# Moving eight adaLN blocks from layer 0's routing to behind its experts

## The reference: what is computed

```python
mod = ada_mod(c, w_ada[i], b_ada[i])                      # silu(c) @ w_ada[i] + b: 6 vectors of 1024
h = modulate(rmsnorm(x, norm_mix[i]), mod[:, 0], mod[:, 1])
x = x + mod[:, None, 2] * mixer(h)
h = modulate(rmsnorm(x, norm_ffn[i]), mod[:, 3], mod[:, 4])
x = x + mod[:, None, 5] * moe(h, w_router, b_router, w_exp_gate[i], w_exp_up[i], w_exp_down[i])
```

## Time and profile before

| | us |
|---|---|
| median of 3 runs | 1343.18 (1340.71 to 1351.53) |
| the profiled execution | 1344.42 |
| its span | 1342.8 |
| PE busy | 1213.2 (90%) |
| DVE, ACT, POOL busy | 371.9, 316.8, 122.9 |
| moved by DMA | 389.56 MB, 290 GB/s over the span |

### The profile page before, as it was taken

One profiled execution on the slowest core, in us unless ns is written; L12 is line 12 of the kernel. 1 busy time (PEld: TensorE's weight loads), 2 busy tenths in 40 slices (PEclk: granted clock), 3 DMA queues, 4 the chain that ended last, 5 costly groups with the idle time before them and its releaser, 6 DMA issues.

```text
span 1342.8 us, 24595 instructions
## 1 busy us (share of the span) xinstructions
PE 1213.2 (90%) x10356; PEld 702.6 (52%) x10356; DVE 371.9 (28%) x1138; ACT 316.8 (24%) x716; POOL 122.9 (9%) x188
## 2 busy tenths in 40 slices
PE   4787998789999989899989999999899987789996
PEld 2345544346886545555547743446465544565544
DVE  1246111250003522611122023341441115551113
ACT  1131111240123531211124211230311114401113
POOL 3001010210000000111120000000002111001111
PEclk8799998999999999899989999999999997989998
DMA  8999999795226793789979223891679989439993
GB/s 316 412 385 421 381 406 421 299 351 174 94 94 243 266 366 107 305 341 409 407 282 354 82 94 104 349 361 64 238 278 421 415 351 363 186 120 410 398 397 137
DMA packets 89707, 389.56 MB, mean 290 GB/s; under 512 B 10456, under 2 KB 38604, under 8 KB 53240
## 3 DMA queue, kind: packets, MB, share of 16 engines
q1 hardware_dynamic: 71568, 336.61, 64.2%
q0 software_dynamic: 17456, 51.07, 10.4%
q10 hardware_dynamic: 568, 0.23, 0.1%
HBM read 370.96 MB, written 27.96 MB: 297 GB/s over the span
## 4 chain that ended last, share of the span: by engine, by line
PE 77%; DMA 10%; DVE 5%; SPq 2%; issue 2%; ACT 2%; POOL 1%; ACTq 0%; POOLq 0%; DVEq 0%
PE bank L478 70%; DMA sb_ring<-in_w_ada 3%; PE bank L941 2%; SPq L435 2%; DMA sb_ring<-in_w_exp_up 2%; DMA slot_out<-sb_arena,sb_homes 1%; DMA sb_ring<-in_w_exp_gate 1%; DMA sb_arena<-slot_out,sb_slots 1%; PE bank L992 1%; PE bank L959 1%; POOL sb_arena L2078 1%; DMA slot_out<-sb_arena 1%; DMA sb_arena<-token_rows,sb_rows 1%; PE bank L874 0%; DVE sb_xT L1937 0%
## 5 line engine op out<-in xcount | busy, mean ns | idle before, releaser
L478 PE MATMUL bank<-sb_ring,sb_arena 128*32 128x256 f32 (+1 forms) x6112 | 460.3, 432 | 18.6 <-DMA sb_ring<-in_w_exp_down 6.4
L478 PEld LDWEIGHTS bank<-sb_ring,sb_arena 128*32 128x32 f32 x6112 | 226.7, 112 | 192.2 <-issue 109.4
L478 PE MATMUL bank<-sb_ring,sb_hT 128*128 128x256 f32 x624 | 142.3, 390 | 6.2 <-ACT sb_hT L1193 6.2
L478 PE MATMUL bank<-sb_arena 128*128 128x128 f32 (+8 forms) x728 | 127.9, 354 | 10.1 <-DVE sb_arena L1826 6.3
L478 PEld LDWEIGHTS bank<-sb_ring,sb_hT 128*128 128x128 f32 x624 | 121.6, 196 | 28.8 <-issue 10.5
L478 PE MATMUL bank<-sb_ring,sb_cond 128*2 128x512 f32 x768 | 104.4, 670 | 18.0 <-DMA sb_ring<-in_w_ada 17.6
L478 PEld LDWEIGHTS bank<-sb_arena 128*128 128x128 f32 (+2 forms) x728 | 90.0, 180 | 43.6 <-issue 13.3
L478 PE MATMUL bank<-sb_arena,sb_ring 128*128 128x384 f32 (+2 forms) x288 | 95.5, 507 | 3.0 <-DVE sb_arena L1678 2.1
L1892 DVE TENSOR_TENSOR sb_arena<-sb_arena,bank 128x256 f32<-128x256 f32 x40 | 16.9, 422 | 274.4 <-PE bank L478 274.4
L478 PE MATMUL bank<-sb_hT,sb_ring 128*128 128x384 f32 x256 | 82.9, 486 | 0.0
L478 PEld LDWEIGHTS bank<-sb_arena,sb_ring 128*128 128x128 f32 (+1 forms) x288 | 49.9, 181 | 44.9 <-issue 19.0
(11 more groups left out here) (310 smaller groups left out, 1029.5 us busy)
## 6 DMA issues: line engine op xcount, KB each, us to landing
sb_ring<-in_w_ada SPq DMA_DIRECT2D x96, 1024.0 KB
sb_ring<-in_w_exp_gate SPq DMA_DIRECT2D x60, 1024.0 KB
sb_ring<-in_w_exp_up SPq DMA_DIRECT2D x60, 1024.0 KB
sb_ring<-in_w_exp_down SPq DMA_DIRECT2D x60, 1024.0 KB
sb_ring<-in_w_mlstm_in SPq DMA_DIRECT2D x12, 1024.0 KB
token_rows<-sb_arena POOLq DMA_DIRECT2D x12, 512.0 KB, 4.7
slot_out<-sb_arena POOLq DMA_DIRECT2D x9, 512.0 KB, 8.5
sb_scratch<-in_w_exp_gate SPq DMA_DIRECT2D x4, 1024.0 KB
```

Of the source, the lines that this page charges most:

```text
L478: return pe.matmul(out, lhsT, rhs, start=first, stop=last)
```

## The change

Group 3 leaves `ADA_WINDOW[0]` and goes to a new table, `ADA_BEHIND[0]`. In the list of units its eight blocks now stand behind the 45 entries of layer 0's experts, and `hold` moves on by eight entries, so that it still falls on the first block of layer 1's mixer. PE does the group inside norm 2: four blocks ahead of the squares, once six of the eight rows of xT are ready; one between the squares and the second sum; three behind it, then the columns. ACT copies the bank after norm 2's 1/sqrt, and DVE makes `mod` and `amp` directly ahead of norm 2's scaling.

```diff
-        ADA_WINDOW = [(3,), (7,), (11,), ()]
+        ADA_WINDOW = [(), (7,), (11,), ()]
+        ADA_BEHIND = [(3,), (), (), ()]
...
-            hold[len(units) + 3 * (NE - 1)] = (yg_in[NT - 1], 32 * (L + 1))
+            hold[len(units) + 3 * (NE - 1) + KC * len(ADA_BEHIND[L])] = (yg_in[NT - 1], 32 * (L + 1))
...
             assert len(units) == moe_first[L] + 3 * (NE - 1)
+            ada_units(*ADA_BEHIND[L])
...
-            def norm(n):
+            def norm(n, groups=()):
+                for g in groups:
+                    pe.wait_ge(x_ready, 8 * n + 6)
+                    ada(g, 0, 1, 2, 3)
                 for k in range(KC):
...
                 ins.then_inc(ms_full, 1)
+                for g in groups:
+                    ada(g, 4)
                 pe.wait_ge(sq_ready, 6 * n + 6)
                 mm(ps[6][:, 0:TOK], mean_ones[:, 32:32 + P], rstd[:, :], True, True).then_inc(ms_full, 1)
+                for g in groups:
+                    ada(g, 5, 6, 7)
+                    ada_columns(g)
...
-                    norm(2 * L)
+                    norm(2 * L, ADA_BEHIND[L - 1])
...
                     norm_scale(2 * L)
+                    for g in ADA_BEHIND[L - 1]:
+                        mod_rows(g)
                 act.wait_ge(mod_added, 3 * L + 1)
...
+                if L:
+                    for g in ADA_BEHIND[L - 1]:
+                        mod_columns(g)
                 norm(2 * L, amp[:, L, 0, :, :])
```

## The result

The changed kernel takes 1365.24 us (1364.54 to 1366.06, 4 runs) against 1342.88 us (1340.71 to 1351.53, 4 runs) for the kernel before on the same chip: a ratio of 1.015, 95% interval 1.0123 to 1.0177, +22.4 us. Timed again beside each other later, the same pair gave 1361.53 (1357.61 to 1368.04, 4 runs) and 1342.38 us (7 runs), 1.0119 (1.006 to 1.0178), +19.2 us. Forecast were 1360.1 us and +16.9. The profiled execution took 1366.06 us, its span is 1364.4.

The account below looks back on a forecast made before the run. The chain that ended last was taken as 77% TensorE and 10% DMA. Terms -4.1 + 0 + 14.5 + 6.5 = +16.9 us on the profiled 1344.4 gave 1361.3, less 1.2 for the median: 1360.1 us, range 1348 to 1367.

Parts of the forecast that it names:

- case A: The forecast itself, all four terms as costed, 66%; own range 1356 to 1366 us.
- Term 1: Layer 0's routing, first position matmul to round 2's gates, gets shorter without the adaLN blocks: -4.1 us (-2.5 to -4.9).
- Term 2: Late gate block ahead of round 8: the 5.0 us wait stays, since loads hang on ring releases; 0 us.
- term 4: Norm 2 of layer 0 pays for group 3's blocks and columns ahead of its scaling: +6.5 us (5.8 to 8).
- term 3: Expert-output gathers behind layer 0's experts share DMA with w_ada; last lands at 280.2, not 265.7: +14.5 us.
- case E: Worse, 5%: w_ada also too late for norm 2, or clock low through it; +22 or more, 1365 to 1370 us.
- the transfer from layer 3: Layer 0's routing stage was to run like layer 3's, which has no adaLN there: 38.70 us instead of 42.84.
- The four blocks ahead of the router: Layer 0, before routing: they end about when hT's last row is ready, so removing them was costed at nothing.
- the dry stretch: DMA at 340 GB/s from 150 to 165 us: queue nearly dry, no early backlog left, loads then follow PE's rounds.
- The even split in bytes: Gathers beside w_ada get half the DMA bytes, not a third: +7.5 us instead of +14.5.
- Rival C: Gathers lose less, 11%: even share of the engines (+7.5) gives 1353.1 us, mere latency (+3.7) 1349.3.

Follow-up runs that it names:

- the kernel before with small blocks: Kernel before, with group 3's eight blocks in their old place but loaded as 64 KB each instead of 1 MB; 1343.48 us, ratio 0.9989.
- the first experiment: Changed kernel, with group 3's eight blocks loaded as 64 KB each instead of 1 MB, the engines' work kept; 1351.59 us, ratio 1.0048.
- the two 1 KB runs: Kernel before without layer 0's hold, mixer weights beside the gathers, 1348.52 us; changed kernel with the eight blocks in 1 KB packets, 1371.35 us.
- under the hold: Changed kernel with hold eight entries earlier, on group 3's first block, so w_ada loads behind the gathers; 1364.96 us, ratio 1.0145.
- the last kernel: Changed kernel with 1 KB packets, four blocks at a time, sixteen matmuls in the routing gap, aside expert's loads at round 4; 1346.84 us, ratio 1.0046.
- the four-group kernel: Changed kernel with group 3's blocks in 1 KB packets, taken four at a time so PE goes round four column groups; 1358.28 us, ratio 1.0118.

## Why the prediction was right or wrong

**Direction and main mechanism were right.** The time is within the range, case A is what happened, and the gathers carry it. The forecast is not saved by terms that cancel: terms 1 and 2 were together 2.6 us too good, term 4 was 1.0 too small, term 3 right. The size was 17 forecast and 19 to 22 measured, the trace's own sum at layer 1's start being 20.4. At 1365.24 us the time also touches case E's, but not by its mechanism: PE waits for no block of w_ada in norm 2, and the clock is back at 0.94 from 284 to 289 us.

**Term 1, -4.1, came out at -1.4.** From the first position matmul to round 2's gates are 144.74 - 103.33 = 41.41 us, 42.84 before. The step that failed is the transfer from layer 3, where the stage takes 38.70. In all seven traces of kernels with this gap left empty layer 0's stage takes 40.7 to 41.7 us. The 2.7 us between them are two things of like size. The idle gap is the same (5.44, 5.45), but the clock was down earlier and for longer, 0.50 over 104 to 112, where the like stretch of layer 3 (1173 to 1181) has 0.60: the picks begin 9.16 us behind the first position matmul and last 9.16, in layer 3 8.24 and 8.46, 1.6 us more. And the token fetch, with 6.06 us shorter than the 9.30 of the earlier trace rows, was still waited for, 1.35 us, though DMA moved only 196 GB/s then; in layer 3 PE doesn't wait for it. One row of another layer didn't bound the phase of the clock, and my bound of -2.5 was too narrow. Of the -1.5 us that are left at POOL's first gather the changed kernel had -1.2 already at the first position matmul (103.33 against 104.53), from 24 matmuls of the mixer near 54 us (6.32 us against 7.62) that the change doesn't touch. The four blocks ahead of the router, put at nothing, did cost nothing: from 60.34 (61.54 before) to the first position matmul both kernels take 42.99 us.

**Term 2, 0, held as to its mechanism.** The wait stays, even with w_ada's bytes gone, and the dry stretch is there again (348 GB/s from 150 to 165, 340 before). It grew from 5.0 to 7.2 us, and the block's way from issue to landing from 16.35 to 18.55. PE's lead was waited away there: it came to the wait at 223.99 - 7.2 = 216.8, before at 224.4 - 5.0 = 219.4, 2.6 us sooner, and left it 0.4 sooner. Why the block doesn't land sooner in proportion stays open (in the kernel before with small blocks it landed 5.1 us sooner, at 219.10, after round 2 had begun 5.2 sooner); the wait was 5.9 us in the first experiment, which has 0.5 MB of w_ada behind it, so the eight blocks' bytes aren't needed for it. The clock behind the wait was 0.74, not 0.50, from 224 to 229, hence 8.35 us of matmuls instead of 9.39.

**Term 3, +14.5, measured +14.4.** Rate and start were right: 1.68 and 0.82 MB in 6 us are 280 and 137 GB/s, forecast from the earlier trace rows were 275 and 138. The landing was forecast at 280.2 and came at 278.61. In the second trace of the changed kernel the gathers take 25.2 us, not 26.6, so about 1.4 us of the term are chance. The even split in bytes that I weighed against the row is refuted by the two 1 KB runs; counted in the profile's packets, the Trainium skill's rule of turns (DMA: Bandwidth & Descriptors, Queues, rings and completion order) is what the traces show. What I didn't see is that w_ada is needed for norm 2 as well. Two kernels let the gathers land early, and won 2.5 and 1.5 us at the scaling. Rival C was priced as if the gain of faster gathers were kept; in these two it was not. Gathers and w_ada together are 8.4 + 2.9 = 11.3 MB, 27 us at 417 GB/s, so from POOL's first gather at 252.03 both can't have landed before about 279 (an estimate, and the changed kernel comes close to it). That bound alone doesn't explain the small gains: in the two kernels w_ada's last block landed at 291.02 and 287.85, 12 and 9 us behind it, since the engines were not full (244 GB/s from 252 to 264 us under the hold; 350 to 354 from 265 to 285 with 1 KB packets). From the last block's matmuls to the scaling are 4.2 us under the hold (291.06 to 295.25). Whether an order exists that gets near 279 + 4 = 283 wasn't tried.

**Term 4, +6.5, measured +7.5.** The four blocks ahead of the squares: the last gather landed to the second mean matmul is 292.32 - 278.61 = 13.71 us, 9.56 before, so +4.2 including the fifth block, where I had 3.2. The clock was 0.50 under the combine (279 to 284 us), and from the first of the four blocks to the squares are 4.3 us (284.90 to 289.22), with a gap of 0.71, not 3.6. The last three and the columns: 5.44 us to the scaling, forecast 5.5. The first experiment has the whole term by itself: 19.3 us from landing to scaling.

**What was overlooked** stands in the windows: not only is something slowed where the eight blocks arrive, the place that they left stays empty. The twelve blocks of the ring are issued by 88.8 us and the next only at 127.35. Before, w_ada's blocks were moved ahead of these, and the last of these under the routing.

## What to carry to other kernels

Weights whose use is late still have a cheap time to be moved: a stretch in which nothing else can be issued, as this one under the routing. Before moving a block in a stream, read GB/s in the window that it leaves as well as in the one that it enters; if the first falls by what the second gains, only latency and order are left to win. Where a gather must run beside a stream, cut the stream into packets smaller than the gather's, but add up all bytes that the next stage needs and ask when the last of them lands: here the gain of 11 us in the gathers became 1.5 us.

## What the runs showed of the hardware

- Two queues on the same DMA engines moved equal numbers of packets and not equal bytes: 227 to 229 with packets of w_ada (bytes 2.0 to 1), 539 to 535 with 1 KB packets (bytes 0.3 to 1), and 590 to 521 and 531 to 528 in the two changed kernels with 1 KB packets.
- The last gather, 5.2 to 5.9 us with nothing large beside it, took 8.7 and 8.8 beside 1 KB packets, and 18.6 to 20.4 beside w_ada's.
- Matmuls with an output of two partitions: 128 of 256 columns in one group of 32 took 26.9 us, in turns over four groups 12.0 us, 9.6 us in the last kernel, both partly at a low clock. At a clock of 0.98 to 1.00, 48 records in one group took 9.66 us and 64 in turns 3.66.
- SP's issues of a 1 MB block take longer with rows of 1 KB than with rows of 8 KB, the shortest 2.1 us against 0.33. The eight w_ada issues spread over 48.9 us (225.09 on) in the four-group kernel, 22.2 us (224.68 on) in the changed one.
